# A three-block transformer kernel on one core: first loads, the end of the program, and the seam between stick-breaking attention and its output projection

## The reference

```
# block 1, two layers
for i in range(2):
    x = x + 0.5 * swiglu_ffn(rms_norm(x, g[0]), w_in[i,0], w_out[i,0])     # D_FF = 2816
    h = rms_norm(x, g[1])
    x = x + (conformer_conv(h, ...) if i == 0 else stick_breaking_attention(h, w_qkv, w_o))
    x = x + 0.5 * swiglu_ffn(rms_norm(x, g[2]), w_in[i,1], w_out[i,1])
x = rms_norm(x, final_g)

# stick-breaking attention, 16 heads of 64, causal
z = q @ k.T / 8;  log_beta = log_sigmoid(z);  log_1m = where(mask, log_beta - z, 0)
suffix = reverse_cumsum(log_1m) - log_1m
a = where(mask, exp(log_beta + suffix), 0);   out = (a @ v) @ w_o

# block 2: two kinds of attention, gated and merged, a convolved feed-forward network, a norm
# block 3: differential attention and a state-space branch, merged; then a mixture of
# 64 experts of hidden width 512, two per token out of a group chosen first
logits = rms_norm(x) @ w_router + b_router
x = x + sum over the two chosen experts of weight * (silu(h @ gate_e) * (h @ up_e)) @ down_e
out = rms_norm(x, final_norm)
```

## Time and profile before

| | us |
|---|---|
| median of 3 runs | 2975.26 |
| lowest and highest | 2972.92, 2978.64 |
| profiled execution | 2981.14 |
| its span, first to last instruction | 2979.3 |

### The profile page before, as it was taken

The page is one execution under the profiler, slowest core; times in us unless marked ns, Lnnn a source line. Parts: engine busy times, 40 slices in busy tenths (PEclk is TensorE's granted clock), DMA queues, the critical chain, the costliest instruction groups (busy, mean ns, idle before and its releaser), DMA issues. The chain is left out here.

```text
span 2979.3 us, 33680 instructions
## 1 busy us (share of the span) xinstructions
PE 2883.6 (97%) x14113; PEld 2240.9 (75%) x14113; DVE 920.7 (31%) x1961; ACT 455.0 (15%) x855; POOL 0.2 (0%) x4
## 2 busy tenths in 40 slices
PE   7999899999999999999999999999997999999997
PEld 6888788888888888898888888888886343434443
DVE  2116721021035210344025417456303222222222
ACT  1001410010024100113010002344201000101011
POOL 0000000000000000000000000000000000000000
PEclk9999999999999999999999999899998999999999
DMA  7444145354443444445644443555462999999996
GB/s 250 142 149 149 56 142 168 128 170 142 147 120 118 138 146 150 124 110 131 159 141 153 158 127 87 149 145 145 121 173 77 425 428 425 427 426 426 426 427 253
DMA packets 369428, 594.32 MB, mean 199 GB/s; under 512 B 15232, under 2 KB 326688, under 8 KB 346656
## 3 DMA queue, kind: packets, MB, share of 16 engines
q1 hardware_dynamic: 363952, 586.09, 56.1%
q10 hardware_dynamic: 5360, 6.55, 0.8%
HBM read 591.52 MB, written 1.08 MB: 199 GB/s over the span
## 5 line engine op out<-in xcount | busy, mean ns | idle before, releaser
L684 PE MATMUL bank<-hR,ring 128*128 128x256 f32 x3520 | 764.2, 380 | 3.1 <-DMA ring<-in_ffn_w_in 3.1
L684 PEld LDWEIGHTS bank<-hR,ring 128*128 128x128 f32 x3520 | 670.7, 191 | 95.2 <-DMA ring<-in_ffn_w_in 3.5
L820 PE MATMUL bank<-big,ring 128*128 128x256 f32 x2016 | 440.8, 382 | 4.9 <-ACT big L1019 4.3
L820 PEld LDWEIGHTS bank<-big,ring 128*128 128x128 f32 x2016 | 385.8, 191 | 59.0 <-issue 4.7
L2732 PE MATMUL bank<-ring,wk 128*64 128x512 f32 x1408 | 312.8, 597 | 5.6 <-DMA ring<-in_w_expert_gate 5.6
L2732 PEld LDWEIGHTS bank<-ring,wk 128*64 128x64 f32 x1408 | 100.0, 138 | 211.5 <-issue 211.2
L719 DVE TENSOR_TENSOR wk<-bank,rstd 128x512 f32<-128x512 f32 x88 | 60.9, 692 | 484.3 <-PE bank L684 483.9
L2758 PE MATMUL bank<-big,wk 128*64 128x512 f32 x352 | 155.8, 595 | 15.1 <-ACT wk L2788 15.1
L2829 DVE TENSOR_TENSOR hT<-bank,hT 128x512 f32<-128x512 f32 x92 | 63.6, 691 | 315.1 <-PE bank L2719 312.8
L856 DVE SCALAR_TENSOR_TENSOR xT<-bank,xT 128x512 f32<-128x512 f32 x36 | 24.9, 692 | 433.2 <-PE bank L820 433.1
L1856 PE MATMUL bank<-big,ring 128*128 128x256 f32 x640 | 141.1, 379 | 1.5 <-ACT big L2326 1.0
(11 more groups left out here) (375 smaller groups left out, 2698.5 us busy)
## 6 DMA issues: line engine op xcount, KB each, us to landing
ring<-in_ffn_w_in SPq DMA_DIRECT2D x88, 1024.0 KB
ring<-in_w_expert_gate SPq DMA_DIRECT2D x44, 2048.0 KB
ring<-in_w_expert_up SPq DMA_DIRECT2D x44, 2048.0 KB
ring<-in_w_in SPq DMA_DIRECT2D x96, 512.0 KB
big<-in_w_expert_down SPq DMA_DIRECT2D x44, 1024.0 KB
ring<-in_ffn_w_out SPq DMA_DIRECT2D x20, 2048.0 KB
ring<-in_w_up SPq DMA_DIRECT2D x22, 1024.0 KB
hR<-in_w_expert_down SPq DMA_DIRECT2D x22, 1024.0 KB
```

The costliest lines, as they stand in the source:

```text
L684: last = nc.tensor.matmul(k.bank[:, n % 4, h * S:(h + 1) * S], w[:, c, h * 256 + m * P:h * 256 + (m + 1) * P], k.hR[:, c, :], start=c == 0 ...
L820: return nc.tensor.matmul(k.bank[:, 4 + o // 2, (o % 2) * S:(o % 2 + 1) * S], w[:, c, o * P:(o + 1) * P], self.src[:, n, :], start=n == 0 ...
```

## The change

Four things are changed.

1. **First loads.** `Setup` loads only the first 256 columns of the constants (identity and ones), under a semaphore of their own. The other 2818 columns, `row` and `pos` are loaded by `Angles`, on SP's queue, behind the 11 units of the first `GatedUp`. PE, ACT and DVE wait for the late constants in `Angles`.
2. **The seam.** In `Stick`, PE now runs `project_v(7)` and 8 matmul calls of the output projection (`begin(0)`: output tiles 0 and 1, input chunks 0 to 3) ahead of `weigh(6)`, and 8 more (`begin(1)`: tiles 2 and 3) between `suffix(7)` and `weigh(7)`. ACT takes the values of group 7 ahead of the output of group 6. These 16 calls are left out behind the fence. The projection's banks are now 0, 7, 4, 5, so that the first two are free during the last groups.
3. **Routing.** Scaling the logits and adding the bias are one instruction for each half of the tokens.
4. **The end.** DVE adds each quarter as soon as its `put` is there, ACT squares each quarter at once (the scale of 1/32 in the square takes the place of the division by 1024), with a square root of one column ahead of it whose only effect is the table; the fences of `Experts` and `FinalNorm` are gone; DVE scales by quarters and SP stores each quarter of 256 KB by itself.

```diff
     def sp(self, sp):
         k = self.k
         sp.dma_start(self.x, k.arg["x"].rearrange("a (t p) n -> p (a t) n", p=P)).then_inc(k.x_loaded, 16)
-        sp.dma_start(k.con[:, :], k.arg["constants"]).then_inc(k.con_loaded, 16)
+        sp.dma_start(k.con[:, 0:FIRST], k.arg["constants"][:, 0:FIRST]).then_inc(self.ones_loaded, 16)
 
...
     def act(self, act, chain):
         k = self.k
         act.dma_start(k.par[:, :], k.arg["params"]).then_inc(k.par_loaded, 16)
-        act.dma_start(k.row[:, :], k.arg["rows"].to_broadcast([P, N_ROW])).then_inc(k.row_loaded, 16)
-        act.dma_start(k.pos[:, :], k.arg["positions_3"].to_broadcast([P, S])).then_inc(k.pos_loaded, 16)
...
     def pe(self, pe):
         k, nc = self.k, self.k.nc
         pe.wait_ge(k.x_loaded, 16)
-        pe.wait_ge(k.con_loaded, 16)
+        pe.wait_ge(self.ones_loaded, 16)
...
     def act(self, act, chain):
         k, nc = self.k, self.k.nc
-        for t in range(T):
-            chain(nc.scalar.activation(k.wk[:, t * DM:(t + 1) * DM], k.x[:, t, :], ACT.Square,
-                                       accum_out=k.ss[:, t:t + 1]), self.squared)
-        act.wait_ge(self.var_ready, self.at(self.var_ready, 1))
-        chain(nc.scalar.activation(k.ss[:, 4:6], k.ss[:, 2:4], ACT.Sqrt), self.root_ready)
+        rounds, per = self.experts.last, 4 * self.experts.PAIRS
+        nc.scalar.activation(k.ss[:, 15:16], k.c("ones")[:, 0:1], ACT.Sqrt)
+
+        def root(t):
+            act.wait_ge(self.var_ready, self.at(self.var_ready, t + 1))
+            nc.scalar.activation(k.ss[:, 8 + t:9 + t], k.ss[:, 4 + t:5 + t], ACT.Sqrt).then_inc(self.root_ready, 1)
+
+        for n in range(4):
+            act.wait_ge(self.experts.put_taken, rounds * per + (4 + n + 1))
+            nc.scalar.activation(k.wk[:, n * 512:(n + 1) * 512], self.quarter(k.x, n), ACT.Square, scale=1.0 / 32,
+                                 accum_out=k.ss[:, n:n + 1]).then_inc(self.squared, 1)
+            if n == 2:
+                root(0)
+        root(1)
+
+    def variance(self, dve, chain, t):
+        k, nc = self.k, self.k.nc
+        dve.wait_ge(self.squared, self.at(self.squared, 2 * t + 2))
+        chain(nc.vector.scalar_tensor_tensor(k.ss[:, 4 + t:5 + t], k.ss[:, 2 * t:2 * t + 1], EPS6, k.ss[:, 2 * t + 1:2 * t + 2],
+                                             ALU.add, ALU.add), self.var_ready)
+
+    def inverse(self, dve, chain, t):
+        k, nc = self.k, self.k.nc
+        dve.wait_ge(self.root_ready, self.at(self.root_ready, t + 1))
+        chain(nc.vector.reciprocal(k.ss[:, 10 + t:11 + t], k.ss[:, 8 + t:9 + t]))
+
+    def scale(self, chain, n):
+        k, nc = self.k, self.k.nc
+        x = self.quarter(k.x, n)
+        chain(nc.vector.scalar_tensor_tensor(x, x, k.ss[:, 10 + n // 2:11 + n // 2], k.r(self.row)[:, (n % 2) * 512:(n % 2 + 1) * 512],
+                                             ALU.mult, ALU.mult), self.scaled)
 
     def dve(self, dve, chain):
-        k, nc = self.k, self.k.nc
-        dve.wait_ge(self.squared, self.at(self.squared, T))
-        chain(nc.vector.tensor_scalar(k.ss[:, 2:4], k.ss[:, 0:2], 1.0 / DM, EPS6, ALU.mult, ALU.add), self.var_ready)
-        dve.wait_ge(self.root_ready, self.at(self.root_ready, 1))
-        chain(nc.vector.reciprocal(k.ss[:, 6:8], k.ss[:, 4:6]))
-        for t in range(T):
-            chain(nc.vector.scalar_tensor_tensor(k.x[:, t, :], k.x[:, t, :], k.ss[:, 6 + t:7 + t], k.r(self.row),
-                                                 ALU.mult, ALU.mult))
+        self.inverse(dve, chain, 0)
+        self.scale(chain, 0)
+        self.variance(dve, chain, 1)
+        self.scale(chain, 1)
...
+        self.scale(chain, 3)
+
+    def sp(self, sp):
+        k = self.k
+        out = k.arg["out"].rearrange("a (t p) n -> p (a t) n", p=P)
+        for n in range(4):
+            sp.wait_ge(self.scaled, n + 1)
+            sp.dma_start(self.quarter(out, n), self.quarter(k.x, n)).then_inc(self.stored, 16)
+        sp.wait_ge(self.stored, 64)
...
+    def one(self, j, c, o):
+        k = self.k
+        w = k.slot(self.slot_of(j), 0, min(4, self.chunks - 4 * j), DM)
+        n = 4 * j + c
+        return k.nc.tensor.matmul(k.bank[:, self.banks[o // 2], (o % 2) * S:(o % 2 + 1) * S], w[:, c, o * P:(o + 1) * P],
+                                  self.src[:, n, :], start=n == 0 and o % 2 == 0, stop=n == self.chunks - 1,
+                                  skip_group_check=True)
+
+    def begin(self, pe, b):
+
+        pe.wait_ge(self.loaded(0), self.loads(0))
+        for o in (2 * b, 2 * b + 1):
+            for c in range(4):
+                self.one(0, c, o)
+
...
+                for o in range(4 if self.begun and j == 0 else 0, KC):
                     last = one(j, c, o)
...
-            nc.vector.scalar_tensor_tensor(x, pair(k.bank[:, 4 + b, :]), self.scale, x, ALU.mult, ALU.add).then_inc(k.x_done, 1)
+            nc.vector.scalar_tensor_tensor(x, pair(k.bank[:, self.banks[b], :]), self.scale, x, ALU.mult, ALU.add).then_inc(k.x_done, 1)
...
             else:
-                weigh(g)
                 if g + 1 < self.G:
                     self.project_v(pe, g + 1)
+                    pe.wait_ge(self.qk_taken, self.G)
+                    pe.wait_ge(self.o_taken, 4)
+                    self.behind.begin(pe, 0)
+                else:
+                    self.behind.begin(pe, 1)
+                weigh(g)
...
-                take_out(g)
                 if g + 1 < self.G:
                     take_v(g + 1)
+                take_out(g)
...
+    def sp(self, sp):
+        k = self.k
+        sp.dma_start(k.con[:, FIRST:], k.arg["constants"][:, FIRST:]).then_inc(k.con_loaded, 16)
+        sp.dma_start(k.row[:, :], k.arg["rows"].to_broadcast([P, N_ROW])).then_inc(k.row_loaded, 16)
+        sp.dma_start(k.pos[:, :], k.arg["positions_3"].to_broadcast([P, S])).then_inc(k.pos_loaded, 16)
+
+    def pe(self, pe):
+        pe.wait_ge(self.k.con_loaded, 16)
...
+        dve.wait_ge(k.con_loaded, 16)
...
         logits = wk[:, 0:144].rearrange("p (t n) -> p t n", t=T)
-        bg = k.r("b_group_router_3").rearrange("p (t n) -> p t n", t=1).to_broadcast([P, T, 8])
-        be = k.r("b_expert_router_3").rearrange("p (t n) -> p t n", t=1).to_broadcast([P, T, 64])
+        a = ROW["b_group_router_3"][0]
+        assert ROW["b_expert_router_3"][0] == a + 8
+        bias = k.row[:, a:a + 72]
         psum = k.bank[:, 5, 0:144].rearrange("p (t n) -> p t n", t=T)
         gl, el = logits[:, :, 0:8], logits[:, :, 8:72]
         for t in range(T):
-            chain(v.tensor_scalar(logits[:, t, :], psum[:, t, :], k.ss[:, 6 + t:7 + t], None, ALU.mult))
-        tt(gl, gl, bg, ALU.add)
-        tt(el, el, be, ALU.add)
+            chain(v.scalar_tensor_tensor(logits[:, t, :], psum[:, t, :], k.ss[:, 6 + t:7 + t], bias, ALU.mult, ALU.add))
...
         chain.leave(n)
-        dve.wait_ge(self.put_ready, n * (4 * m) + 4)
-        take_put()
-        chain.sem = self.tail_chain
-        chain(v.memset(k.small[:, 39:40], 0.0))
-
-
...
-    def act(self, act, chain):
-        k = self.k
-        act.dma_start(k.arg["out"].rearrange("a (t p) n -> p (a t) n", p=P), k.x[:, :, :]).then_inc(self.stored, 16)
-        act.wait_ge(self.stored, 16)
+        for j in range(4):
+            dve.wait_ge(self.put_ready, n * (4 * m) + (j + 1))
+            take_quarter(j).then_inc(self.put_taken, 1)
+            if j == 2:
+                chain.sem = self.tail_chain
+                self.final.variance(dve, chain, 0)
...
-            plan += [Stick(k, "stick", norm, k.hR, a["attn_w_qkv"][0], 0, DM, 2 * DM), Project(k, "swo", big, KC, a["attn_w_o"][0])]
+            stick = Stick(k, "stick", norm, k.hR, a["attn_w_qkv"][0], 0, DM, 2 * DM)
+            stick.behind = Project(k, "swo", big, KC, a["attn_w_o"][0], banks=(0, 7, 4, 5), begun=True)
+            plan += [stick, stick.behind]
```

More of the change, by code:

```diff
@@ L78 @@
 CONST_ARRAY = np.ascontiguousarray(np.concatenate(_parts, 1))
+FIRST = 2 * P
+assert CONST["ident"][1] <= FIRST and CONST["ones"][1] <= FIRST
 PARAM_NAMES = ["norm_g", "conv_b_pw1", "conv_w_dw", "conv_b_dw", "conv_ln_g", "conv_ln_b",
@@ L308, in name_sems @@
         self.turned = sem("turned")
+        self.ones_loaded = sem("ones_loaded")
     def __init__(self, k, name):
@@ L2630 @@
     PAIRS = 2
+    fence = False
     def name_sems(self, sem):
@@ L2781, in act @@
         act.wait_ge(self.route.eid_ready, 1)
-        with act.Fori(0, self.rounds(act)) as i:
+        n = self.last = self.rounds(act)
+        with act.Fori(0, n) as i:
             for s in range(self.PAIRS):
@@ L2824, in take_tokens, with take_quarter @@
                 chain(last, self.xg_taken if b else None)
+        def take_quarter(n):
+            x = k.x[:, n // 2, (n % 2) * 512:(n % 2 + 1) * 512]
+            return v.tensor_tensor(x, k.bank[:, self.PUT_BANKS[n], :], x, ALU.add)
         def take_put():
-            for n, bank in enumerate(self.PUT_BANKS):
```

(4 more changed lines are left out.)

34 lines of the change are left out of this document (17 added, 17 removed).

## The result

The changed kernel took 2953.95 us, the median of six runs (2951.81 to 2954.87); the kernel before, run beside it six times, took 2974.51 us. The ratio is 0.9926, with a 95% interval of 0.9913 to 0.9939: faster by 22 us. The forecast was 2950.6 us and 24.7 us faster. The profiled execution took 2953.32 us, 27.8 us less than the profiled one of before.

What follows compares the result with a forecast made beforehand. PE is busy nearly throughout, so only its waits and the ends can give time: 6.0 + 10.7 + 0.5 + 7.5 = 24.7 us off the median 2975.26 gives 2950.6 us, range 2943 to 2962.

Steps and rivals of the forecast that it cites:

- first loads: At the start: fewer bytes ahead of the first weight unit, which lands near 13.9 instead of 19.93; gain 6.0 us.
- seam: Last two attention groups and output projection: earlier start 0.9, moved records 6.9, clock 2.9; gain 10.7 us, bounds 7.3 and 11.5.
- routing: In the routing's DVE chain: two bias sums gone; gain 0.5 us, bounds 0.2 and 0.55.
- end: After the last put: sums, squares, scaling and stores by quarters; gain 7.5 us, bounds 5.6 and 8.2.
- the lower bound: First loads gain only 4.9 us: the dip to 85 GB/s stays and x still lands 7.4 us from issue.
- that loss of some 3 us: PE's slow start (transposes, 3 us idle, first unit) was taken to stay, with 1.7 us either way.
- cover of 41 us: Late loads delay the output projection's first unit, issued at 134.35 and first used at 175.60, so they should cost nothing.
- slack of 0.35 us: At the seam: work put ahead of `suffix(7)` ends at 964.3, before its earliest start at 964.65.
- the term for the clock: At the projection's start: 7 us at mean clock 0.58 lose 2.9 us, recovered once the idle times are filled.
- rival (d): PE drops to 1.2 GHz at the new order and stays there through the projection: 10 us slower, 2985.5; chance 0.03.
- the handovers: In the end's DVE chain: seven handovers between instructions, estimated at 0.05 us each.

Runs made afterwards that it cites:

- part alone: The kernel before with only that part of the change: start 0.9981 (mean 2971.96 us), seam 0.9970 (2967.9 us), end 0.9970 (2968.5 us).
- the second profile of before: The kernel before, profiled once more with no edit: 2975.01 us, in a span of 2973.2 us.
- the first comparison: Six runs of the changed kernel beside six of the kernel before: medians 2953.95 and 2974.51 us, ratio 0.9926.

## Why the prediction was right

| term | forecast | in the profiles | part alone, in means |
|---|---|---|---|
| first loads | 6.0 | 6.5 | 5.9 |
| seam | 10.7 | 10.4 | 10.0 |
| routing | 0.5 | 0.5 | not run |
| end | 7.5 | 7.6 | 9.4 (7.7 in its trace) |
| sum | 24.7 | 25.0 | 25.8 |

**First loads.** Bytes at the measured rate was the right rule. The dip to 85 GB/s went with the long constants, as assumed, and x landed after 6.3 us; the lower bound had it keep its 7.4. The transposes moved by 5.61 us, less than the 6 forecast, and the idle time in front of the first unit shrank by 0.85 us where I had it stay, hence 13.46 instead of 13.9. "I leave that loss of some 3 us as it is, with 1.7 us either way": the loss stayed on average and changed from execution to execution, and in the profiled one it was 2.8 us smaller than in the profile of before. The late loads cost nothing, as their cover of 41 us said.

**The seam.** The projection started 0.88 us earlier for 0.9. From the projection's start to the next network were 20.82 us against 30.38, 9.56 less, for 6.9 + 2.9 = 9.8 forecast; with useless work in place of moved work that was 27.73, so 6.9 are the records and 2.65 the clock. The slack of 0.35 us at `suffix(7)` held, with a wait of 0.30 us for the mask. What the step didn't say is that the term for the clock isn't a constant of the kernel: in the second profile of before it was 2.2 us smaller, with full pace in `project_v(7)` behind an idle time of 3.22 us. So slow work doesn't follow each such idle time, as I had read from one profile, and a part of the term's good fit is the luck of that profile. The remark to rival (d), that low stretches end within 7 us of PE being busy, holds for the seam alone. From 1885 to 1900 us in before PE is busy for 14.42 of 15 us at a mean clock of 0.54.

**Routing.** PE's wait is 0.53 us shorter, for 0.5 forecast. No run has this part alone.

**The end.** Scaling was done 8.14 us after the last `put` began, 8.2 forecast, and the span ended 2.79 us later, 2.8 forecast. The two small errors cancel: a scaling of a quarter takes 0.75 us instead of 0.65, since 512 columns cost more than half of 1024, and the handovers took less than seven times 0.05. The estimate after the Trainium skill, "DMA: Bandwidth & Descriptors", Anatomy of one DMA, 2.6 us for a quarter, agrees with the 2.7 us from issue to landing. The page gives its rule for DMAs that GpSimd issues, and these are SP's, so the agreement bears out the estimate and not the page.

**The sum.** The difference in the first comparison is 20.6 us between the medians and 22 by the ratio, 24.7 was forecast, and the median came out at 2953.95 instead of 2950.6. The six runs of before in that comparison have a median of 2974.51, on the lower of its two levels, while most of its 51 later runs lie on the upper. Over all runs the difference is 23.6 to 24.7 us. That the two profiled executions lie 27.8 us apart is luck the other way, with 2.76 us of it in the first unit alone. About 1.5 us are lost at the low clock near 2095 us, which no step had.

## What to carry to other kernels

Where a short idle time of PE recurs in a dependent chain, later independent work put into it gains twice: its own time, and the clock behind it, which here also let the chain start earlier. Ask of each gap whether slow records follow it, and whether PE is what ends last there, for in the routing, 20 us at the low clock were worth 0 to 0.4 us by the last `put`. Of the first loads only what the first instructions read should stand ahead of the first weights, and the first unit of weights can be split so that PE starts on a half. One profile holds one draw of the clock; the gain is read part by part between fixed points of the two traces, and the whole from many runs.

## What the runs showed that I had not expected

- The same kernel has two levels 6 us apart, which differ by where the low clock falls, and the same place loses 1.7 us at the low clock in one execution and 2.6 in the next, with the same idle time of 3 us ahead.
- Sixteen transposes that are the first work of PE take 3.3 to 3.65 us, and 1.98 us when useless multiplications run ahead of them. The granted clock tells nothing of it: the table by stretches has 6 records in a microsecond of the changed kernel and 12 in the same one behind useless work, both at 1.00. Here the changed kernel:

```profile
8.00:9.00 1.00, 1.00 (x6) 1.00 (x6) 0.34 (x1) 0.00 (x0) 0.00 (x0) 1.00 1.09 345
```

  And with useless work ahead of the transposes:

```profile
8.00:9.00 1.00, 1.00 (x12) 1.00 (x11) 0.81 (x2) 0.20 (x1) 0.00 (x0) 1.00 1.09 374
```

- Filling the routing's idle times raised the mean granted clock of the profiled execution from 0.990 to 0.996 and gave 1.7 us in the means, which isn't resolved; the start's useless work and the split unit raised it to 0.992 and gave 7.1. The mean clock says little about what can be gained.
- Time gained ahead of a stage that streams weights can be lost again in it: the 1.5 us of the first experts were gone by the last `put`.
